# Decoder trunk on one core: the norm's guess from one ScalarE activation, and another order of the last norm

## The reference

```
for layer in range(2):
    hn = rms_norm(h, norm_mix[layer])
    h = h + (mixer_ab if layer == 0 else mixer_c)(hn, ...)
    h = h + conv_ffn(rms_norm(h, norm_ffn[layer]), ...)
return rms_norm(h, norm_final)

rms_norm(x, g) = x * rsqrt(mean(x * x) + 1e-6) * g
conv_ffn: z = h @ w_up (5632 wide), causal width-3 conv, silu(gate) * up, @ w_down
```

## Time and profile before

| | us |
|---|---|
| median of 3 runs | 2197.65 |
| lowest, highest | 2195.17, 2197.65 |
| profiled execution, its time | 2193.04 |
| profiled execution, its span | 2191.2 |
| busy: PE, PEld | 2128.9, 1738.1 |
| busy: DVE, ACT, POOL | 1484.0, 887.5, 880.4 |
| mean granted TensorE clock | 0.991 |

### The profile page before, as it was taken

One profiled execution on the slowest core, in us unless ns is written; L12 is line 12 of the kernel. 1 busy time (PEld: TensorE's weight loads), 2 busy tenths in 40 slices (PEclk: granted clock), 3 DMA queues, 4 the chain that ended last, 5 costly groups with the idle time before them and its releaser, 6 DMA issues.

```text
span 2191.2 us, 26108 instructions
## 1 busy us (share of the span) xinstructions
PE 2128.9 (97%) x10128; PEld 1738.1 (79%) x10128; DVE 1484.0 (68%) x1679; ACT 887.5 (41%) x1127; POOL 880.4 (40%) x458
## 2 busy tenths in 40 slices
PE   8998999989989999999999999999899999999996
PEld 5886788778868888888888888888688888888885
DVE  6669755463686676777698912436877766686987
ACT  4221233343454444444443532025544444444445
POOL 4323211122267777674000333333777777730000
PEclk9999999999999999999999999999999999999998
DMA  4101000003222222222988211113221222239872
GB/s 164 39 29 39 27 14 29 20 21 115 87 77 87 87 87 87 81 83 90 368 319 288 77 39 39 39 48 119 82 80 67 86 87 87 87 111 381 303 261 77
DMA packets 93916, 236.09 MB, mean 108 GB/s; under 512 B 9937, under 2 KB 10210, under 8 KB 93794
## 3 DMA queue, kind: packets, MB, share of 16 engines
q1 hardware_dynamic: 92642, 230.23, 29.4%
q10 hardware_dynamic: 1152, 4.19, 0.5%
HBM read 198.73 MB, written 35.65 MB: 107 GB/s over the span
## 4 chain that ended last, share of the span: by engine, by line
PE 69%; DVE 4%; ACT 2%; issue 1%; POOL 1%; DVEq 0%; ACTq 0%; POOLq 0%
PE ps L1164 12%; PE ps L1165 11%; PE ps L1166 11%; PE ps L1200 6%; PE ps L1201 6%; PE ps L1198 6%; PE ps L772 3%; PE ps L778 3%; PE ps L775 3%; PE ps L1261 1%; PE ps L1262 1%; PE ps L1263 1%; DVE act_lo L1350 1%; PE ps L1310 1%; DVE t_lo L1705 1%
## 5 line engine op out<-in xcount | busy, mean ns | idle before, releaser
L581 POOL TENSOR_TENSOR w_hi<-w_raw,ones 128x1024 fp32r<-128x1024 f32 x56 | 111.8, 1997 | 799.8 <-PE ps L778 242.3
L1164 PE MATMUL ps<-t_hi,w_hi 128*128 128x512 f32 x672 | 265.4, 395 | 8.0 <-ACT snap L2212 4.8
L1165 PE MATMUL ps<-t_lo,w_hi 128*128 128x512 f32 x672 | 263.0, 391 | 0.0
L1166 PE MATMUL ps<-t_hi,w_lo 128*128 128x512 f32 x672 | 262.6, 391 | 0.0
L627 POOL TENSOR_TENSOR w_lo<-w_sum,w_hi 128x1024 fp32r<-128x1024 f32 x84 | 232.8, 2782 | 23.1 <-ACT w_hi L2215 23.1
L1198 PE MATMUL ps<-d_hi 128*128 128x512 f32 x616 | 240.2, 390 | 0.0
L1201 PE MATMUL ps<-d_hi,d_lo 128*128 128x512 f32 x616 | 239.7, 389 | 0.0
L1200 PE MATMUL ps<-d_lo,d_hi 128*128 128x512 f32 x616 | 239.7, 389 | 0.0
L627 POOL TENSOR_TENSOR w_lo<-w_raw,w_hi 128x1024 fp32r<-128x1024 f32 x84 | 158.3, 1885 | 199.3 <-ACT w_hi L2215 181.5
L1164 PE MATMUL ps<-act_hi,w_hi 128*128 128x512 f32 x504 | 196.8, 390 | 4.6 <-ACT snap L2212 4.6
L1166 PE MATMUL ps<-act_hi,w_lo 128*128 128x512 f32 x504 | 196.6, 390 | 0.0
(11 more groups left out here) (290 smaller groups left out, 4599.9 us busy)
## 6 DMA issues: line engine op xcount, KB each, us to landing
w_raw<-w_up SPq DMA_DIRECT2D x44, 1024.0 KB, 4.9
d_ring<-w_dn SPq DMA_DIRECT2D x146, 256.0 KB, 7.8
d_ring<-g_kept SPq DMA_DIRECT2D x124, 256.0 KB, 9.2
g_kept<-gst SPq DMA_DIRECT2D x44, 512.0 KB, 2.6
w_raw<-w_in SPq DMA_DIRECT2D x24, 512.0 KB, 3.6
chain_a<-g_kept SPq DMA_DIRECT2D x44, 256.0 KB, 8.9
x_kept<-x SPq DMA_DIRECT2D x16, 512.0 KB, 8.7
x<-x_kept SPq DMA_DIRECT2D x16, 512.0 KB, 10.1
```

The lines of the kernel that those rows point to most:

```text
L581: pool.tensor_tensor(w_hi[:, slot, :], w_raw[:, parity, :], ones[:, 0:1].to_broadcast([P, 1024]), ALU.mult).then_inc(s_whi, 1)
L1164: pe.matmul(out, wh, bh, start=(fresh and j == 0), stop=False, skip_group_check=True)
L1165: pe.matmul(out, wh, bl, start=False, stop=False, skip_group_check=True)
L1166: ins = pe.matmul(out, wl, bh, start=False, stop=(j == 3), skip_group_check=True)
```

## The change

It touches every norm.

- The variance operation of DVE is gone. ACT reads the sum from PSUM in a single activation, `Abs_reciprocal_sqrt` with scale 1/D and a bias tile holding eps, in place of Ln and Exp (`guess`, `last_guess`).
- The refinement keeps three DVE operations, now t = (sum + D eps) y, v = (-0.5/D) t y, y = (v + 1.5) y. The first reads PSUM, and `norm.var` counts the first two. The waits of PE for `norm.var` 1 are as they were.
- In `residual` the refinement stands behind the four `low34`, as before; the variance operation ahead of them is gone.
- The mixer C norm has its sum in banks 2 and 3, value tile 5 moves from bank 2 to bank 7, and the rstd by position goes to bank 3.
- In the tail, half 0's guess stands ahead of item 4 of half 1 instead of behind it; DVE refines half 0 before the second addition; the third addition stands behind three scalings of half 0 and the fourth behind seven; the last square is not accumulated by DVE but added by PE with a second matmul of ones.

```diff
--- before.py
+++ after.py
@@ -211,7 +211,7 @@
         def past(count, n):
             return count.sem, count.first + n
 
-        PER_NORM = {"sq": KT, "acc": KT - 1, "hi": KT, "lo": KT, "sum": 1, "var": 3, "ln": 1, "exp": 1, "rstd": 1}
+        PER_NORM = {"sq": KT, "acc": KT - 1, "hi": KT, "lo": KT, "sum": 1, "guess": 1, "var": 2, "rstd": 1}
         Norm = namedtuple("Norm", ("col", *PER_NORM))
         norm_sems = {name: sem("norm_" + name) for name in PER_NORM}
         BY_TILE = ("sq", "acc", "hi", "lo")
@@ -408,7 +408,7 @@
                 self.added = sem(f"last{h}_added")
                 self.sum = sem(f"last{h}_summed")
                 self.step = sem(f"last{h}_vector_steps")
-                self.guess = sem(f"last{h}_ln_exp")
+                self.guess = sem(f"last{h}_guessed")
                 self.gained = sem(f"last{h}_gained")
                 self.out = sem(f"last{h}_out")
         L = [LastSem(0), LastSem(1)]
@@ -423,7 +423,7 @@
         s_rope_v = sem("rope_vector_steps")
         s_rope_a = sem("rope_scalar_steps")
 
-        V_BANKS = (4, 5, 6, 0, 1, 2)
+        V_BANKS = (4, 5, 6, 0, 1, 7)
         WO_SLOT = (0, 1, 2, 3, 0, 1, 0, 1)
         SLOT = (3, 2, 0, 1)
         CU_SLOT = (3, 2)
@@ -1232,8 +1232,12 @@
                     last_sum(1)
 
             def last_sum(h):
-                pe.wait_ge(*past(f1.hacc[h], KT - 1))
-                pe.matmul(ps[:, 4 + h, :], ones[:], acc[:, LAST[h]], start=True, stop=True).then_inc(L[h].sum, 1)
+                pe.wait_ge(*past(f1.hacc[h], KT - 1 - h))
+                ins = pe.matmul(ps[:, 4 + h, :], ones[:], acc[:, LAST[h]], start=True, stop=(h == 0))
+                if h:
+                    pe.wait_ge(*past(f1.hsq[h], KT))
+                    ins = pe.matmul(ps[:, 4 + h, :], ones[:], sq[:, (KT - 1) % 2, LAST[h]], start=False, stop=True)
+                ins.then_inc(L[h].sum, 1)
 
             ffn(f0, norms[1], WO)
 
@@ -1243,7 +1247,7 @@
                 n = 8 * half + st
                 bank = V_BANKS[n % 6]
                 if n < 6 and ks[0] == 0:
-                    pe.wait_ge(*past(f0.xadd, (16, 16, 16, 17, 17, 18)[n]))
+                    pe.wait_ge(*past(f0.xadd, (16, 16, 16, 17, 17, 16)[n]))
                 if n == 4:
                     pe.wait_ge(CN.lo, 2 * KT)
                 if n >= 6 and ks[0] == 0:
@@ -1273,13 +1277,13 @@
             for h in range(2):
                 pe.wait_ge(*past(f0.hacc[h], KT - 1))
             for h in range(2):
-                ins = pe.matmul(ps[:, 3 + 4 * h, :], ones[:], acc[:, LAST[h]], start=True, stop=True)
+                ins = pe.matmul(ps[:, 2 + h, :], ones[:], acc[:, LAST[h]], start=True, stop=True)
             ins.then_inc(norms[2].sum.sem, 1)
             v_tile(0, 3)
             v_tile(0, 4)
             pe.wait_ge(*past(norms[2].rstd, 1))
             for st in range(ST):
-                ins = pe.matmul(ps[:, 7, st:st + 1], rstd[0:1, st * P:(st + 1) * P], ones[0:1, 0:1], start=True, stop=True)
+                ins = pe.matmul(ps[:, 3, st:st + 1], rstd[0:1, st * P:(st + 1) * P], ones[0:1, 0:1], start=True, stop=True)
             ins.then_inc(C.rn, 1)
 
             for k in range(0, KT, 2):
@@ -1322,19 +1326,14 @@
 
                 dve.memset(carry[:, j:j + 1], 0.0)
 
-            def norm_var(norm, psum):
-
-                dve.wait_ge(*past(norm.sum, 1))
-                dve.tensor_scalar(sq[:, 0, :], psum, 1.0 / D, EPS, ALU.mult, ALU.add).then_inc(norm.var.sem, 1)
-
-            def norm_refine(norm):
+            def norm_refine(norm, psum):
 
                 v, t = sq[:, 0, :], sq[:, 1, :]
-                dve.wait_ge(*past(norm.exp, 1))
-                dve.scalar_tensor_tensor(t, v, -0.5, rstd[:], ALU.mult, ALU.mult).then_inc(norm.var.sem, 1)
+                dve.wait_ge(*past(norm.guess, 1))
+                dve.scalar_tensor_tensor(t, psum, D * EPS, rstd[:], ALU.add, ALU.mult).then_inc(norm.var.sem, 1)
+                dve.wait_ge(*past(norm.var, 1))
+                dve.scalar_tensor_tensor(v, t, -0.5 / D, rstd[:], ALU.mult, ALU.mult).then_inc(norm.var.sem, 1)
                 dve.wait_ge(*past(norm.var, 2))
-                dve.tensor_tensor(v, t, rstd[:], ALU.mult).then_inc(norm.var.sem, 1)
-                dve.wait_ge(*past(norm.var, 3))
                 dve.scalar_tensor_tensor(rstd[:], v, 1.5, rstd[:], ALU.add, ALU.mult).then_inc(norm.rstd.sem, 1)
 
             def accumulate(norm, k):
@@ -1351,13 +1350,13 @@
                                          act_hi[:, k, :].bitcast(F32), ALU.mult, ALU.subtract).then_inc(norm.lo.sem, 1)
 
             dve.memset(ones[:], 1.0).then_inc(s_setup, 1)
+            dve.memset(tiny[:, 61:62], EPS).then_inc(s_setup, 1)
             dve.memset(glT[0:32, :], 1.0).then_inc(s_rope_v, 1)
             for k in range(KT):
                 act_low(norms[0], k)
             for k in range(KT):
                 accumulate(norms[0], k)
-            norm_var(norms[0], slot2(2))
-            norm_refine(norms[0])
+            norm_refine(norms[0], slot2(2))
 
 
             dve.wait_ge(B.gl, 1)
@@ -1721,10 +1720,9 @@
                 accumulate(norm, KT - 2)
                 accumulate(norm, KT - 1)
                 combine(3)
-                norm_var(norm, slot2(0))
                 for j in range(4):
                     low34(j)
-                norm_refine(norm)
+                norm_refine(norm, slot2(0))
 
             residual(WO, R_WO, norms[1], f0, 0)
 
@@ -1893,12 +1891,9 @@
             ffn(f0, 0, norms[1], norms[2], False)
 
 
-            dve.wait_ge(*past(norms[2].sum, 1))
-            dve.tensor_scalar(sq[:, 0, :].rearrange("p (b n) -> p b n", b=2), ps[:, 3:8:4, :], 1.0 / D, EPS, ALU.mult, ALU.add
-                              ).then_inc(norms[2].var.sem, 1)
-            norm_refine(norms[2])
+            norm_refine(norms[2], slot2(1))
             dve.wait_ge(C.rn, 1)
-            dve.tensor_copy(tiny[:, 20:28], ps[:, 7, 0:8]).then_inc(C.rnf, 1)
+            dve.tensor_copy(tiny[:, 20:28], ps[:, 3, 0:8]).then_inc(C.rnf, 1)
             dve.wait_ge(s_cmx, 16 * 2)
             dve.tensor_tensor(wst[:], wst[:], cst[:, None, C_TRIL:C_TRIL + P].to_broadcast([P, KT, P]), ALU.mult).then_inc(C.ws, 1)
 
@@ -1958,19 +1953,15 @@
                 dve.wait_ge(*past(f1.xadd, 9 + m // 2))
                 dve.tensor_tensor(x[:, m, LAST[1]], x[:, m, LAST[1]], ps[:, m, :], ALU.add).then_inc(L[1].added, 1)
 
-            def last_var(h):
-                dve.wait_ge(L[h].sum, 1)
-                dve.tensor_scalar(sq[:, 0, LAST[h]], ps[:, 4 + h, :], 1.0 / D, EPS, ALU.mult, ALU.add).then_inc(L[h].step, 1)
-
             def last_refine(h):
                 v, t, y = sq[:, 0, LAST[h]], sq[:, 1, LAST[h]], rstd[:, LAST[h]]
-                dve.wait_ge(L[h].guess, 2)
-                dve.scalar_tensor_tensor(t, v, -0.5, y, ALU.mult, ALU.mult).then_inc(L[h].step, 1)
+                dve.wait_ge(L[h].guess, 1)
+                dve.scalar_tensor_tensor(t, ps[:, 4 + h, :], D * EPS, y, ALU.add, ALU.mult).then_inc(L[h].step, 1)
+                dve.wait_ge(L[h].step, 1)
+                dve.scalar_tensor_tensor(v, t, -0.5 / D, y, ALU.mult, ALU.mult).then_inc(L[h].step, 1)
                 dve.wait_ge(L[h].step, 2)
-                dve.tensor_tensor(v, t, y, ALU.mult).then_inc(L[h].step, 1)
+                dve.scalar_tensor_tensor(y, v, 1.5, y, ALU.add, ALU.mult).then_inc(L[h].step, 1)
                 dve.wait_ge(L[h].step, 3)
-                dve.scalar_tensor_tensor(y, v, 1.5, y, ALU.add, ALU.mult).then_inc(L[h].step, 1)
-                dve.wait_ge(L[h].step, 4)
 
             def last_scale(h, items):
                 cols = LAST[h]
@@ -1981,32 +1972,28 @@
 
             for i in range(4):
                 half_accumulate(f1, 1, i)
-            for m in range(4):
-                last_add(m)
-                if m:
-                    half_accumulate(f1, 1, m + 3)
-                if m == 0:
-                    last_var(0)
-                elif m == 1:
-                    last_refine(0)
-                    last_scale(0, range(3))
-                elif m == 2:
-                    last_scale(0, range(3, 5))
-            half_accumulate(f1, 1, KT - 1)
-            last_var(1)
-            last_scale(0, range(5, KT))
+            last_add(0)
+            half_accumulate(f1, 1, 4)
+            last_refine(0)
+            last_add(1)
+            half_accumulate(f1, 1, 5)
+            last_scale(0, range(3))
+            last_add(2)
+            half_accumulate(f1, 1, 6)
+            last_scale(0, range(3, 7))
+            last_add(3)
+            last_scale(0, range(7, KT))
             last_refine(1)
             last_scale(1, range(KT))
 
 
         @block.scalar
         def _(act):
-            def guess(norm):
-
-                act.wait_ge(*past(norm.var, 1))
-                act.activation(rstd[:], sq[:, 0, :], ACT.Ln).then_inc(norm.ln.sem, 1)
-                act.wait_ge(*past(norm.ln, 1))
```

(24 more changed lines are left out.)

## The result

The changed kernel takes 2206.66 us (median of 7 runs, 2203.03 to 2210.26), the kernel before 2197.64 in the same runs (median of 7): a ratio of 1.0045, 95% interval 1.0036 to 1.0055. By the interval of the ratio the change makes the kernel 8 to 12 us slower (the medians differ by 9.0), where I had forecast 6. A second set of runs gave 1.0044 (1.0030 to 1.0057).

What follows compares the result with a forecast made beforehand. PE, busy 97% of the span, was taken to bound the kernel. Terms 4.1 + 4.1 + 0 + 0 - 2.1 = +6.1 us on the median 2197.65 gave 2203.8; range 2196.5 to 2207.5, the forecast's own 2200.8 to 2205.4.

Steps and rivals of the forecast that it cites:

- FFN entries: At each entry PE stalls 6.6 us ahead of pair 1, and its restart moves by +4.1 us (2.6 to 4.9).
- P5: FFN entry product, fourth of 12 matmuls each, needed by the third snapshot; forecast to end at 641.4, snapshot 4.1 us later.
- POOL goes first: At the FFN entry, waiting POOL runs ahead of DVE's fourth low34, which then ends at 627.25.
- The second entry costs +4.1 too: Second FFN entry has the first's schedule 927.32 us later, so it also loses 4.1 us.
- behind it PE runs without a wait, so nothing takes this back: After PE's restart at 654.85 in the FFN entry, the +4.1 us delay stays.
- First norm: First refinement operation ends at 44.65, before PE wants the bank at 44.91: 0, at most +0.3 us.
- Mixer C norm: rstd comes earlier than 1271.03, PE reads it at 1273.38, nobody waits: 0.
- Tail: Behind PE's last projection matmul, the eight scalings start at 2181.2 instead of 2183.30: -2.1 us (-3.1 to 0).
- both low-clock stretches at their long end, no gain in the tail: Rival 3, FFN entries and tail: 2 x 4.9 + 0 = +9.8 us, 2207.5; chance 0.09.
- DVE keeping its place: Rival 1, FFN entries: POOL gets in behind the fourth low34, stall 4.3 us, total +0.7, 2198.4; chance 0.17.
- the four `low34` as one string: Rival 2, FFN entries: DVE runs them uninterrupted, stall 2.0 us, total -6.5, 2191.1; chance 0.12 with partial forms.
- The faster outcome: Whole kernel faster than before, through DVE getting the SBUF side at the FFN entries; chance 0.11.

Runs made afterwards that it cites:

- the added wait: Changed kernel with ACT's high_b(1) also waiting for the third low34, at both FFN entries: 2203.41 us, ratio 1.0028 to the kernel before.
- the first profile: First profiled execution of the changed kernel, 2205.53 us; the second profile is of the same kernel run again, median 2208.27 us, ratio 1.0044.
- the first experiment: Changed kernel with the first refinement operation behind the first low34 instead of the fourth at both FFN entries: 2194.63 us, ratio 0.9987 to the kernel before.

## Why the prediction was wrong, point by point

- **FFN entries: the mechanism right, the second entry too small.** Predicted a wait of 6.6 us, released by the first refinement operation, and +4.1 each; the traces have 6.18 and +4.3 and +4.6. The last `low34` at 3.4 us, the third snapshot later (4.3 us against PE's schedule, predicted 4.1) and starting as P5 ends, the first entry's second wait unchanged: all as stated. That POOL goes first was argued from one row and is now shown by the added wait.
- **"The second entry costs +4.1 too", a term sized too small.** The prediction took the second entry to be the first one again, because its first matmul of the pairs stood 927.32 us behind. That held up to the third snapshot. But before, PE's wait at the restart was 3.41 us in the first entry and 1.42 in the second, with the clock low behind the first (47.4 us) and high behind the second (45.8). In six of seven profiles of the new norms the second has the low clock too. So the second entry cost 4.6 in the first profile and 6.0 in the second, and "behind it PE runs without a wait, so nothing takes this back" missed that something is added.
- **First norm: the step that failed.** "First refinement operation to 44.65, and PE wants the bank at 44.91: 0, at most +0.3." The working took the table load to be over, as it had been at 31 us before. The diff has *two* waits ahead of that activation (the second for the eps tile), and the load came behind them, 1.28 us in the open: 1.3 us on PE. The other guesses have one wait each; there the load stood ahead of the wait (the mixer C norm, load at 1264.20, activation at 1270.62), or the sum was there by the time of the load, or, for the last half, no load was needed.
- **Mixer C norm: right.** No wait of PE for it.
- **Tail: right.** -2.1 predicted; -2.5 to the scalings, -2.1 to -2.5 to the end. The addition of tile 3 came later, as worked out (1.2, predicted 1.35); the second sum matmul took 1.70, between the two ends. One load is left of four.
- **The total.** With the first norm's 1.3 put in, the prediction's sum is +7.4; the measured terms make +7.7 in the first profile and +9.5 in the second, against 8 to 12 measured (9.9 by the ratio). So of the 3.8 us that the forecast was short the first norm has 1.3 and the second entry 0.5 to 1.9; 0.4 to 2.2 us of the measured loss are in no term and stay open. The measured ratio times the median shown gives 2207.54, just past the top of my range (2207.5) and above the forecast's own part of it (to 2205.4), whose upper bound had nothing in it for either term: the range reached that far only through a rival (both low-clock stretches at their long end, no gain in the tail) that is not what happened.
- **The rivals.** DVE keeping its place, and the four `low34` as one string, are excluded by the rows above. The faster outcome was there to be had, by another mechanism than I gave it: with `rstd` early *and* the bank freed in time an entry gains 3.4 us up to the restart and 1.1 to 2.7 in all.

## What to carry to other kernels

Where a shorter chain replaces a longer one, look for who used an intermediate step of the old chain as a signal: here the removed operation also told PE that a bank was free, and its successor stood behind four others. A freed 1.2 us slot on an engine whose operations exclude another's is worth nothing if the other takes it, and a request that now comes at another time can collide. Look in the trace where a table load stands: with two waits ahead of its activation it fell behind them here. And a gap closed at one place can leave a longer wait, and a low clock, at the next: count an entry past its last restart.

## What the runs showed of the hardware

- Where the load stands depends on the waits in the program: with two waits ahead it started at 42.46, behind an idle time of 11.38 us, with one at 31.36, for the same activation.
- DVE operations that read PSUM and at most one SBUF tile kept 1.21 us beside POOL's operations (L1331 at 622.56 in the first experiment, L1328 at 617.95 before), where those with two SBUF tiles took 2.3 to 3.4. The Trainium skill says so too ("SBUF — State Buffer", section "Who interferes with whom": outside the 2-port perf modes, a DVE instruction with at most one SBUF input does not contend with GpSimd), and the traces agree.
- Two profiles of code that was the same up to there, but for two set-up instructions, differed by 5.8 us in PE's schedule at the first FFN entry, 3.4 of them lost to a granted clock of 0.5; two profiles of identical code differed by 1.8. One profile's difference of a few us means nothing until a second profile has it too; the stretches at the entries reproduced within 0.3 us where PE's gaps were the same, but for one entry at 38.0.
- Counted over both entries of the nine profiles, PE's restart came after 3.06 to 4.3 us of waiting in fifteen cases, and the granted clock was 0.5 behind fourteen of them (not behind the one with 3.06 us); it came after 1.4 to 1.8 us in three, and the clock was 1.00 there.
